# A streaming encoder layer: a third pair of score banks, one bank for turned weights, one for outputs, and sums made before the matmul

## The chip, the cores and the metric

The kernel runs on one core of a Trainium2 chip. The metric is the device time of one execution in microseconds, lower is better; 593.93 us is the median of three runs before the change. Of a core's engines, PE does matmuls (PEld are its weight loads), ACT activations and copies, DVE vector work, POOL further vector work and indirect transfers, SP issues most transfers. PE writes to PSUM, eight banks of 512 float32 columns in 128 partitions. Each engine runs its own program in order and waits on counts (semaphores) that the others raise.

## The reference, cut to what matters

```python
h = rmsnorm(x, g_mix); proj = h @ w_in            # GLU value and gate, q, k, v
a_out = silu(layernorm(causal_dwconv(u_hist, conv_w, conv_b), ln_g, ln_b))   # 512 channels, 31 taps
# stick-breaking attention, 8 heads of 64, blocks of 128 queries:
z = einsum(q, k) * scale
later = cumsum(log_keep, reverse=True) - log_keep   # log_keep = log sigmoid(-z) where visible
w = where(vis, exp(log_sigmoid(z) + later), 0);  o = w @ v
b_out = head_rmsnorm(o, g_sb)
x = x + concat(a_out, b_out) @ w_out
x = x + hier_moe(rmsnorm(x, g_ffn), ...)            # 32 experts
```

There are 528 prompt positions (16 learned ones and 512) and 32 new positions of a running stream with 1024 cached ones: with padding 576 columns. Keys and values of the prompt, of the new positions, and the last 30 convolution inputs are outputs too.

## The kernel before, in words

The input projection ends at about 143.7 us, the attention stage follows, and from about 248 us the output projection, the router and 32 experts.

**Attention steps.** `groups` (L415) lists 21 steps, s0 to s20; a step holds two heads. Group 0 is s0 to s3, 128 queries by 128 keys, two heads of the four blocks `i` each. Group 1 holds the few-query steps: s4 and s5 (the last 16 prompt queries: their own 32 keys, then 512), s6, s7 and s8 (the 32 new ones: their own, then twice 512 cached keys). Groups 2, 3 and 4 are s9 to s12 with 256 keys, s13 to s16 with 384, s17 to s20 with 512. `order` (L418) sets them in a row with three turns of keys for output (`ko`) and the three matmul parts of the LayerNorm (mean, variance, spread): 27 places, `q` = 0 to 26. All engines walk through these places.

**One step.** At its place PE makes scores (`scores`, L1013) into two banks; places use banks 0-1 and 2-3 in turn, so place q waits in `bank_free` for the weights of place q-2. ACT makes sigmoid(z) into SBUF and sigmoid(-z) in place (`shares`, L1558). DVE scans the second for the running products and multiplies (`weights`, L1886; the last product, L1908, frees the banks). Two places later (`TURN_LAG`) PE turns both heads' weights into banks 4 and 5 (`turn_weights`, L1042), ACT copies them to SBUF in one instruction (`copy_weights`, L1575), and three places later (`SUM_LAG`) PE multiplies them with the values into bank 6 or 7 (`weigh`, L1059). Four places after a group's last step ACT squares its outputs out of PSUM (`output_squares`, L1594) and DVE sums the squares by head (`head_means`, L1910); POOL makes the root (`head_root`, L741); six places after, DVE scales (`heads_normed`, L1916); seven after, PE turns the result (`turn_out`, L1088) and DVE takes it into the mixed input of the output projection (`outputs_in`, L1926), at the end of its place.

**Work beside it.** The convolution's taps are split: 98 by DVE (94 before the stage, one in each of the places 0 to 3), 26 by POOL (`tap`, L725). For POOL's, ACT makes the product (`product`, L1608), `PRODUCTS[q]` of them at place q, into four buffers: product n waits until POOL has used product n-4. `POOL_TAPS` says how many taps POOL makes before each of the first three head roots: 8, then 10, then 7, and one behind the third. The last four taps write the convolution's result `yc` (L738, L739). The mean (L1108) waits for all of them: eight matmul calls with a matrix of -1 sum four channel blocks in PSUM; DVE subtracts (L1871), ACT squares, 20 calls sum the squares by column (`variance`, L1118), POOL takes the root, PE spreads it, DVE scales (L1882), and at the place behind the last step ACT makes four Silus into the mixed input (L1634).

**The cached keys** are turned by PE at places 0 to 2 into banks 4 to 7 (`turn_ck`, L984) and copied by ACT and DVE, two blocks at a time.

**The way out.** At places 27 and 28 PE runs the first four blocks (attention's half, `LATE`) of the output projection of chunk 0, in two parts, between the last turns and weighings, then the other four, which need the Silus, then chunk by chunk. SP waits for the four Silus to load the first experts' weights, for the last weighing to load the router and more, and for w_out until s8 has been weighed.

## Time and profile before

| | |
|---|---|
| median of 3 runs | 593.93 us (593.9 to 594.14) |
| the profiled execution | 592.3 us, its span 590.6 us |
| mean granted clock of PE | 0.945 |
| PE, DVE, ACT, POOL busy | 527.3, 281.3, 155.7, 98.3 us |

In 40 slices of the span (14.77 us each; digits are tenths of busy time, 9 is 90% or more; PEclk the granted clock in tenths):

```profile
PE   6999999999767799899999799899999877988993
PEld 5779999999545568754555654344343322323330
DVE  2862999999687843714266851111112111001157
ACT  4513122223779832710211201111111111101112
POOL 2100000000657702011002111111112111011002
PEclk9999999999779885999999699999999999889997
DMA  8904745301504400069921789999999999999994
```

The tenth to the seventeenth slice hold the attention stage. A row of a timeline gives start, length, engine, line, operation, what it writes and reads, shape and count, and in brackets the idle time before it with what ended it. PE's matmuls of float32 appear as two passes each (eight calls, 16 passes); transposes as one.

### The profile page before, as it was taken

The numbers are of one execution on the slowest core, as the hardware profiler recorded it, in microseconds if no ns is written. First come the engines' busy times: TensorE is split into PE (matmuls) and PEld (weight loads), VectorE is DVE, ScalarE is ACT, GpSimd is POOL, SyncE is SP. The second block draws the span as 40 slices with busy tenths as digits, with TensorE's granted clock in tenths as the row PEclk, the third lists the DMA queues.
The fourth block names the chain that finished last, engine by engine and source line by source line (L and its number), as shares of the span: only waits on it lengthen the run. The fifth ranks groups of instructions, "written<-read, shape, count | busy, mean of one in ns | idle before, by whom it ended". The sixth has DMA issues, their size and how long they took to land.

```text
span 590.6 us, 7920 instructions
## 1 busy us (share of the span) xinstructions
PE 527.3 (89%) x3189; PEld 336.0 (57%) x3190; DVE 281.3 (48%) x481; ACT 155.7 (26%) x267; POOL 98.3 (17%) x120
## 2 busy tenths in 40 slices
PE   6999999999767799899999799899999877988993
PEld 5779999999545568754555654344343322323330
DVE  2862999999687843714266851111112111001157
ACT  4513122223779832710211201111111111101112
POOL 2100000000657702011002111111112111011002
PEclk9999999999779885999999699999999999889997
DMA  8904745301504400069921789999999999999994
GB/s 295 224 3 149 237 150 168 119 1 43 215 1 158 171 1 0 1 213 424 353 98 59 280 319 427 423 419 421 424 426 425 425 422 423 419 418 422 406 348 158
DMA packets 44764, 148.95 MB, mean 252 GB/s; under 512 B 7124, under 2 KB 23532, under 8 KB 36279
## 3 DMA queue, kind: packets, MB, share of 16 engines
q1 hardware_dynamic: 40263, 139.63, 61.2%
q0 software_dynamic: 4464, 8.80, 3.9%
q8 instruction: 26, 0.43, 0.3%
q14 instruction: 11, 0.09, 0.0%
HBM read 136.29 MB, written 19.59 MB: 264 GB/s over the span
## 4 chain that ended last, share of the span: by engine, by line
PE 60%; DMA 20%; DVE 8%; SPq 4%; issue 4%; ACT 3%; POOL 1%; DVEq 0%; POOLq 0%; ACTq 0%
PE ps L945 17%; DMA big<-in_w_expert_out 12%; PE ps L1170 9%; PE ps L1355 8%; PE ps L1380 5%; DMA cw<-h_dram,low 4%; PE ps L910 3%; PE ps L1071 2%; DVE ps L1895 2%; SPq L632 2%; DMA big<-y_dram 2%; PE ps L1336 2%; PE ps L1125 1%; DMA y_dram<-cw,low 1%; PE ps L898 1%
## 5 line engine op out<-in xcount | busy, mean ns | idle before, releaser
L2168 DVE TENSOR_TENSOR low<-low,ps 128x256 f32<-128x256 f32 x16 | 6.7, 421 | 172.0 <-ACT low L1688 172.0
L1355 PE MATMUL ps<-big,low 128*64 128x512 f32 x320 | 85.0, 593 | 3.3 <-issue 2.3
L945 PE MATMUL ps<-cw_r 128*128 128x280 f32 x256 | 72.3, 292 | 0.0
L1835 DVE SCALAR_TENSOR_TENSOR big<-low,cwt,big 128x590 f32<-128x590 f32 x94 | 72.1, 833 | 0.3
L945 PE MATMUL ps<-low_r,cw_r 128*128 128x280 f32 x256 | 72.2, 292 | 0.0
L945 PE MATMUL ps<-cw_r,big_r 128*128 128x280 f32 x256 | 72.1, 291 | 0.0
L1380 PE MATMUL ps<-big,low 128*64 128x512 f32 x160 | 47.0, 629 | 11.6 <-DMA big<-in_w_expert_out 4.8
L1170 PE MATMUL ps<-cw,low 128*128 128x512 f32 x128 | 56.7, 594 | 0.0
L1355 PEld LDWEIGHTS ps<-big,low 128*64 128x64 f32 x320 | 29.8, 137 | 45.6 <-issue 45.5
L736 POOL TENSOR_TENSOR big<-big 128x590 f32<-128x590 f32 x22 | 28.9, 1335 | 114.7 <-DVE big L1835 106.5
L945 PEld LDWEIGHTS ps<-cw_r 128*128 128x128 f32 x256 | 47.2, 188 | 0.4 <-issue 0.4
L945 PEld LDWEIGHTS ps<-cw_r,big_r 128*128 128x128 f32 x256 | 47.3, 188 | 0.0
L945 PEld LDWEIGHTS ps<-low_r,cw_r 128*128 128x128 f32 x256 | 47.2, 188 | 0.0
L1699 ACT ACTIVATE cw<-ps,low 128x1024 f32<-128x1024 f32 x16 | 17.8, 1115 | 98.2 <-PE ps L1380 98.2
L1355 PE MATMUL ps<-low 128*64 128x512 f32 x128 | 42.3, 593 | 0.2 <-issue 0.2
L1170 PEld LDWEIGHTS ps<-cw,low 128*128 128x128 f32 x128 | 23.6, 190 | 26.3 <-issue 26.3
L1688 ACT ACTIVATE low<-ps 128x256 f32<-128x256 f32 x16 | 6.2, 384 | 107.8 <-PE ps L1355 107.8
L716 POOL TENSOR_TENSOR stat<-stat,nhalf 128x1 f32<-128x1 f32 (+2 forms) x16 | 15.2, 953 | 114.4 <-DVE stat L2013 38.8
L1380 PEld LDWEIGHTS ps<-big,low 128*64 128x64 f32 x160 | 14.8, 144 | 31.6 <-issue 31.6
L798 POOL DMA_INDIRECT cw<-h_dram,low x16 | 16.5, 1034 | 94.7 <-PE ps L1336 83.1
L810 POOL DMA_INDIRECT y_dram<-cw,low x15 | 15.2, 1012 | 100.7 <-ACT cw L1699 87.3
L1895 DVE TENSOR_TENSOR_SCAN ps<-ps,negs 128x128 f32<-128x128 f32 (+4 forms) x36 | 25.4, 750 | 13.7 <-ACT ps L1573 8.9
(265 smaller groups left out, 829.3 us busy)
## 6 DMA issues: line engine op xcount, KB each, us to landing
big<-in_w_expert_in SPq DMA_DIRECT2D x16, 2048.0 KB, 18.1
big<-in_w_expert_out SPq DMA_DIRECT2D x20, 1024.0 KB, 25.3
big<-in_w_in SPq DMA_DIRECT2D x20, 512.0 KB, 5.1
low<-in_w_expert_out SPq DMA_DIRECT2D x8, 1024.0 KB, 29.8
low<-in_w_expert_in SPq DMA_DIRECT2D x4, 2048.0 KB, 22.3
cw<-in_w_expert_in SPq DMA_DIRECT2D x4, 2048.0 KB, 25.7
low<-in_w_expert_in SPq DMA_DIRECT2D x4, 1536.0 KB, 21.7
big<-in_w_expert_in SPq DMA_DIRECT2D x6, 1024.0 KB, 32.4
```

The lines of the kernel that those rows point to most:

```text
L716: pool.tensor_tensor(t, t, nhalf[0:t.shape[0], :].broadcast_to(list(t.shape)), ALU.pow).then_inc(rstd_ready, 1)
L736: pool.tensor_tensor(conv[:, i, :], t, conv[:, i, :], ALU.add).then_inc(pool_tap_done, 1)
L798: pool.indirect_dma_start(out=xg_of(g), out_offset=None, in_=h2_dram, in_offset=bass.IndirectOffsetOnAxis(ap=rows_of[:, g, 0:1].bitcast(U3 ...
L810: pool.indirect_dma_start(out=y_dram, out_offset=bass.IndirectOffsetOnAxis(ap=rows_of[:, g, 1:2].bitcast(U32), axis=0), in_=yg[b], in_offs ...
L910: mm = pe.matmul(ps[:, 4 + c % 2, :], h[:, k, cols], wts[:, k, :], start=m == 0 and k == 0, stop=m == 2 and k == KD - 1, skip_group_check= ...
L945: return pe.matmul(ps[:, proj_bank(j) + half, 0:PROJ], w[:, k, :], h[:, k, cols], start=first, stop=last, skip_group_check=True)
L1170: mm = pe.matmul(ps[0:w, OUT_BANK[c] + n, :], mixt[:, k, P * c:P * c + w], wout[:, k, 512 * n:512 * n + 512], start=k == LATE[0], stop=k = ...
L1355: mm = pe.matmul(ps[TILE * half:TILE * half + TILE, gu_bank(g), :], xt[:, k, TILE * half:TILE * half + TILE], wi_at(2 * g + half, k), star ...
L1380: mm = pe.matmul(ps[TILE * half:TILE * half + TILE, 4 + m, :], gact_t[:, k, TILE * half:TILE * half + TILE], wo[(2 * g + half) % WO_SLOTS] ...
L1699: act.activation((yg_end if g == PAIRS - 1 else yg[b]).rearrange("p (m n) -> p m n", m=2), ps[:, 4:6, :], ACT.Copy, scale=tab[:, g, 2:3]). ...
L1835: ins = dve.scalar_tensor_tensor(conv[:, i, :], u[:, i, j:j + CW], cwt[:, i, j:j + 1], conv[:, i, :], ALU.mult, ALU.add)
L1895: dve.tensor_tensor_scan(k, k, nones[:, 0:1].broadcast_to([P, n]), carry[:, a:a + 1] if cached else 1.0, ALU.mult, ALU.max).then_inc(left_ ...
```

## The change

What it does:

- A score place has three pairs of banks (0-1, 2-3, 4-5), `q % 3`: place q waits for place q-3. Bank 6 holds turned weights and turned outputs, bank 7 the outputs.
- The four turns of cached keys become places of their own, between s0 to s3: 31 places. New places: s0 to s3 at 0, 2, 4, 6, cached keys at 1, 3, 5, 7, `ko` at 8, 14, 19, s4 to s8 at 9 to 13, s9 to s12 at 15 to 18, s13 to s16 at 20 to 23, mean 24, s17 25, s18 26, variance 27, s19 28, spread 29, s20 30. In each such place ACT copies one block and DVE the other.
- Weights are turned three places behind, weighed four behind. With 384 or 512 keys a step's heads are turned one by one, each after the copy of the one before; ACT's copies come between its sigmoids, at the places behind the last step after the Silus.
- ACT copies a group's outputs from bank 7 to SBUF five places behind, and squares and scaling work there. Squares and their sums five behind, scaling seven, outputs eight, and `outputs_in` now comes ahead of the weights in DVE's place. The turn of outputs waits until all turned weights are copied; a turn of weights behind it waits until DVE has taken the outputs.
- DVE sums the four blocks of `yc`, and later of the squares, into one (`summed`); the mean is two matmul calls, the variance five.
- `POOL_TAPS` is (8, 9, 6), three taps stay behind the third root; `PRODUCTS` is one at places 0 to 13, then 2, 1, 1, 1, 1, 2, 1, 1, 1, 1.

```diff
 STEP_TAPS = 4
-POOL_TAPS = (8, 10, 7)
-PRODUCTS = (1, 1, 1, 1, 2, 1, 1, 2, 1, 1, 2, 2, 1, 2, 1, 2, 1, 1, 1, 1)
-TURN_LAG, SUM_LAG = 2, 3
-SQUARE_LAG, MEANS_LAG, NORM_LAG, OUT_LAG = 4, 4, 6, 7
+POOL_TAPS = (8, 9, 6)
+PRODUCTS = (1,) * 14 + (2, 1, 1, 1, 1, 2, 1, 1, 1, 1)
+TURN_LAG, SUM_LAG = 3, 4
+COPY_LAG, MEANS_LAG, NORM_LAG, OUT_LAG = 5, 5, 7, 8
+Z_SLOTS = 3
+TURN_BANK, O_BANK = 6, 7
...
         ln_mean, ln_var, ln_spread = dict(ln="mean"), dict(ln="variance"), dict(ln="spread")
-        order = groups[0] + [dict(ko=0)] + groups[1] + [dict(ko=1)] + groups[2] + [dict(ko=2)] + groups[3]
+        order = [entry for n, st in enumerate(groups[0]) for entry in (st, dict(ck=n))] + [dict(ko=0)] + groups[1] + [dict(ko=1)] + groups[2] + [dict(ko=2)] + groups[3]
         order += [ln_mean] + groups[4][0:2] + [ln_var, groups[4][2], ln_spread, groups[4][3]]
         NQ = len(order)
...
         for q, st in enumerate(order):
-            st["q"], st["bank"] = q, 2 * ((NQ - 1 - q) % 2)
+            st["q"], st["bank"] = q, 2 * (q % Z_SLOTS)
+        turned = 0
+        for st in steps:
+            st["turns"] = [(0, 1)] if st["n"] <= 256 else [(0,), (1,)]
+            st["turn"] = turned
+            turned += len(st["turns"])
+        NT = turned
         for g, sts in enumerate(groups):
             for n, st in enumerate(sts):
                 st.update(g=g, first=n == 0, last=n == len(sts) - 1)
         group_end = [sts[-1]["q"] for sts in groups]
-        O_BANK = (6, 7, 6, 7, 6)
...
-            def turn_weights(st):
-
-                s, n = st["s"], st["n"]
+            def turn_weights(st, part):
+
+                s, n, t = st["s"], st["n"], st["turn"] + part
                 pe.wait_ge(w_ready, s + 1)
-                if s:
-                    pe.wait_ge(wtt_ready, s)
+                if t:
+                    pe.wait_ge(wtt_ready, t)
                 else:
-                    pe.wait_ge(ckt_ready[0], 2)
+                    pe.wait_ge(qk_done, 8)
+                if part == 0 and st["turned_out"]:
+                    pe.wait_ge(mixb_ready, st["turned_out"])
                 w = wts[s % 4]
...
                 pe.wait_ge(onorm_ready, g + 1)
+                pe.wait_ge(wtt_ready, turned_before(g))
...
-                pe.wait_ge(yc_ready, NI)
-                pe.wait_ge(pool_tap_done, NI * TAPS - taps_by_dve)
-                for i in range(NI):
-                    for half in range(2):
-                        mm = pe.matmul(ps[:, st["bank"] + half, 0:HALF], nones[:, :], yc[:, i, HALF * half:HALF * half + HALF],
-                                       start=i == 0, stop=i == NI - 1, skip_group_check=True)
+                pe.wait_ge(sums_ready, 1)
+                for half in range(2):
+                    mm = pe.matmul(ps[:, st["bank"] + half, 0:HALF], nones[:, :], ysum[:, HALF * half:HALF * half + HALF],
+                                   start=True, stop=True)
                 mm.then_inc(mean_done, 1)
 
             def variance(st):
 
                 bank_free(st["q"])
-                for i in range(NI):
-                    pe.wait_ge(devsq_ready, i + 1)
-                    for c in range(NC):
-                        lo = min(P * c, COLS - P)
-                        mm = pe.matmul(ps[:, st["bank"], c:c + 1], lnsq[:, i, lo:lo + P], nones[:, 0:1],
-                                       start=i == 0 and c == 0, stop=i == NI - 1, skip_group_check=True)
+                pe.wait_ge(sums_ready, 2)
+                for c in range(NC):
+                    lo = min(P * c, COLS - P)
+                    mm = pe.matmul(ps[:, st["bank"], c:c + 1], sqsum[:, lo:lo + P], nones[:, 0:1],
+                                   start=c == 0, stop=True, skip_group_check=True)
...
+                early, late = step_at(q - TURN_LAG), step_at(q - SUM_LAG)
+                if early:
+                    turn_weights(early, 0)
+                if late:
+                    weigh(late)
+                if early and len(early["turns"]) == 2:
+                    turn_weights(early, 1)
...
-            def output_squares(g):
+            def copy_out(g):
 
                 act.wait_ge(av_done, groups[g][-1]["s"] + 1)
+                if g == 0:
+                    act.wait_ge(y_cleared, 16 * 9)
+                if g >= 2:
+                    act.wait_ge(o_turned, g - 1)
+                n = 256 if g == 1 else 512
+                o = ot if g == 1 else osb[g % 2]
+                act.copy(o, ps[:, O_BANK, 0:n]).then_inc(o_copied, 1)
+                act.wait_ge(o_copied, g + 1)
                 if g >= 1:
                     act.wait_ge(onorm_ready, g)
-                n = 256 if g == 1 else 512
-                act.activation(osq[:, 0:n], ps[:, O_BANK[g], 0:n], ACT.Square, scale=HD ** -0.5).then_inc(osq_ready, 1)
+                act.activation(osq[:, 0:n], o, ACT.Square, scale=HD ** -0.5).then_inc(osq_ready, 1)
...
-                if group_at(q - SQUARE_LAG) is not None:
-                    output_squares(group_at(q - SQUARE_LAG))
-                if step_at(q):
-                    shares(step_at(q))
-                    if q in (0, 1):
-                        copy_ck(2 * q)
+                if group_at(q - COPY_LAG) is not None:
+                    copy_out(group_at(q - COPY_LAG))
+                st, early = step_at(q), step_at(q - TURN_LAG)
+                if st and len(st["turns"]) == 1:
+                    shares(st, (0, 1))
+                elif st:
+                    shares(st, (0,))
                 elif q < NQ and "ko" in order[q]:
                     copy_ko(order[q])
+                elif q < NQ and "ck" in order[q]:
+                    copy_ck(order[q])
+                if early and q < NQ:
+                    copy_weights(early, 0)
+                if st and len(st["turns"]) == 2:
+                    shares(st, (1,))
...
-                if step_at(q - TURN_LAG):
-                    copy_weights(step_at(q - TURN_LAG))
+                if early and q >= NQ:
+                    copy_weights(early, 0)
+                if early and len(early["turns"]) == 2:
+                    copy_weights(early, 1)
...
+            def summed(total, t):
+
+                dve.tensor_reduce(total, t.rearrange("p i t -> p t i"), AX.X, ALU.add).then_inc(sums_ready, 1)
+
+            carried = [0]
             for q in range(NQ + OUT_LAG + 1):
                 if group_at(q - NORM_LAG) is not None:
                     heads_normed(group_at(q - NORM_LAG))
+                if group_at(q - OUT_LAG) is not None:
+                    outputs_in(group_at(q - OUT_LAG))
                 if step_at(q):
                     weights(step_at(q))
-                    if q in (0, 1):
-                        copy_ck(2 * q + 1)
+                elif q < NQ and "ck" in order[q]:
+                    copy_ck(order[q])
                 elif q < NQ and order[q] is ln_mean:
+                    dve.wait_ge(yc_ready, NI)
+                    dve.wait_ge(pool_tap_done, NI * TAPS - taps_by_dve)
+                    summed(ysum, yc)
                     deviations(order[q])
                 elif q < NQ and order[q] is ln_var:
+                    dve.wait_ge(devsq_ready, NI)
+                    summed(sqsum, lnsq)
                     variances(order[q])
                 elif q < NQ and order[q] is ln_spread:
                     normed(order[q])
```

## Rows read from the trace of the kernel before

**Rows 1.** Windows: us, engines' busy time (instructions), granted clock, DMA share, GB/s.

```profile
178.00:192.00 14.00, 10.30 (x193) 7.77 (x193) 9.99 (x16) 12.97 (x23) 10.52 (x10) 1.00 0.47 169
206.80:213.50 6.70, 6.70 (x18) 4.91 (x19) 0.00 (x0) 0.00 (x0) 0.00 (x0) 0.61 0.00 0
224.40:248.40 24.00, 22.20 (x139) 19.63 (x140) 13.32 (x14) 9.65 (x14) 3.08 (x3) 0.76 0.00 1
```

**Rows 2.** Waits, 143 to 250 us: us in total, times, longest.

```profile
DVE ps L1895 <- ACT ps L1573: 14.8, 6, 4.1
```

**Rows 3.** Timeline, from the scores of s20 into the first output projection.

```profile
241.97 1.13 PE L1019 MATMUL ps<-low 64*128 64x512 f32 x4
...
243.36 0.60 ACT L1572 ACTIVATE big<-ps 128x512 f32<-128x512 f32 x1 [3.77 <-PE ps L1022]
243.85 0.60 ACT L1573 ACTIVATE ps<-ps 128x512 f32<-128x512 f32 x1
...
246.41 1.28 ACT L1634 ACT_TABLE_LOAD   x1
...
246.44 2.00 PE L1071 MATMUL ps<-low,big 128*128 128x64 f32 x16 [1.80 <-ACT big L1582]
...
247.70 3.14 ACT L1634 ACTIVATE low<-big,vt 128x576 f32<-128x576 f32 x4
...
251.76 1.04 PE L1056 MATMUL ps<-ident,big 128*128 128x128 f32 x8
...
257.81 7.08 PE L1170 MATMUL ps<-cw,low 128*128 128x512 f32 x16
```

**Rows 4.** Timeline, from the last instruction of s16 to the deviations.

```profile
205.03 0.96 DVE L1908 TENSOR_TENSOR big<-ps,big 128x766 f32<-128x766 f32 x1
205.33 1.12 POOL L738 TENSOR_TENSOR big<-big 128x528 f32<-128x528 f32 x1
...
206.41 0.25 POOL L739 TENSOR_TENSOR big<-big 128x32 f32<-128x32 f32 x1
...
206.80 6.67 PE L1114 MATMUL ps<-big,negs 128*128 128x288 f32 x16 [1.01 <-POOL big L739]
...
213.50 2.75 DVE L1871 SCALAR_TENSOR_TENSOR big<-ps,big 128x576 f32<-128x576 f32 x4 [6.92 <-PE ps L1114]
```

**Rows 5.** Timeline of DVE: last instruction of s8, then of s12.

```profile
177.64 1.22 DVE L1908 TENSOR_TENSOR big<-ps,big 128x1022 f32<-128x1022 f32 x1
...
190.63 0.69 DVE L1908 TENSOR_TENSOR big<-ps,big 128x510 f32<-128x510 f32 x1
```

**Rows 6.** Lines of POOL: ns min/median/max, first and last start.

```profile
L736 POOL TENSOR_TENSOR big<-big x22: 1222/1334/1446, 148.9 to 194.2; 128x590 f32<-128x590 f32 x22
...
L746 POOL TENSOR_SCALAR stat_h<-stat_h x4: 240/241/245, 167.2 to 259.4; 128x8 f32<-128x8 f32 x4
...
L748 POOL TENSOR_TENSOR stat_h<-stat_h,nhalf x4: 1665/1666/1680, 167.5 to 259.7; 128x8 f32<-128x8 f32 x4
```

**Rows 7.** Groups of ACT by form in the attention stage.

```profile
L1613 ACT ACTIVATE big<-low,cwt 128x590 f32<-128x590 f32 x26 | 19.9, 789 | 0.0
...
L1582 ACT COPY big<-ps 128x512 f32<-128x512 f32 x4 | 2.3, 578 | 0.0
```

**Rows 8.** Lines of DVE: ns min/median/max, first and last start.

```profile
L1914 DVE TENSOR_REDUCE stat_h<-big x4: 675/676/687, 166.4 to 258.6; 128x8 f32<-128x512 f32 x4
L1914 DVE TENSOR_REDUCE stat_o<-big x1: 408/408/408, 188.4 to 188.4; 128x4 f32<-128x256 f32 x1
...
L2006 DVE TENSOR_TENSOR low<-x,low x10: 1068/1088/1100, 275.8 to 325.5; 128x512 f32<-128x512 f32 x8, 64x512 f32<-64x512 f32 x2
```

**Rows 9.** Timeline around the end of s18's weights.

```profile
218.73 2.39 ACT L1604 ACTIVATE big<-big 128x576 f32<-128x576 f32 x4
...
224.18 8.64 PE L1125 MATMUL ps<-negs,big 128*128 128x1 f32 x40
...
225.21 1.22 DVE L1908 TENSOR_TENSOR big<-ps,big 128x1022 f32<-128x1022 f32 x1
```

More of the change, by code:

```diff
@@ L437, in group_at, with turned_before @@
             return group_end.index(q) if q in group_end else None
+        def turned_before(g):
+            return sum(len(st["turns"]) for st in steps if st["q"] + TURN_LAG <= group_end[g] + OUT_LAG)
+        for st in steps:
+            st["turned_out"] = sum(end + OUT_LAG < st["q"] + TURN_LAG for end in group_end)
         def mixed(c):
@@ L1005, in bank_free @@
                     pe.wait_ge(ko_ready, gone["ko"] + 1)
+                elif "ck" in gone:
+                    for r in range(2):
+                        pe.wait_ge(ckt_ready[r], gone["ck"] + 1)
                 elif gone is ln_mean:
@@ L1060, in weigh @@
                 s, g, n, w = st["s"], st["g"], st["n"], wtt[st["s"] % 2]
-                pe.wait_ge(wtt_ready, s + 1)
-                if st["first"]:
-                    if g < 2:
-                        pe.wait_ge(ckt_ready[1], 2)
-                    else:
-                        pe.wait_ge(mixb_ready, g - 1)
+                pe.wait_ge(wtt_ready, st["turn"] + len(st["turns"]))
+                if st["first"] and g:
+                    pe.wait_ge(o_copied, g)
                 if "qb" in st:
@@ L1182, in _ @@
                         turn_ko(order[q])
+                    elif "ck" in order[q]:
+                        turn_ck(order[q])
                     elif order[q] is ln_mean:
@@ L1549, in _, with copy_ck, shares @@
                     upper(9 + 2 * i + HSLOTS)
-            def copy_ck(n):
-                b = 6 - 2 * n
+            def copy_ck(st):
+                n = st["ck"]
+                b = 7 - 2 * n
                 act.wait_ge(ck_turned, n + 1)
-                for a in range(2):
-                    ins = act.copy(ckt[:, :, P * b + P - P * a:P * b + 2 * P - P * a],
-                                   ps[:, 4 + a, :].rearrange("p (i t) -> p i t", i=NI))
-                ins.then_inc(ckt_ready[0], 1)
-            def shares(st):
+                act.copy(ckt[:, :, P * b:P * b + P],
+                         ps[:, st["bank"], :].rearrange("p (i t) -> p i t", i=NI)).then_inc(ckt_ready[0], 1)
+            def shares(st, heads):
                 s, n, bank = st["s"], st["n"], st["bank"]
-                act.wait_ge(z_ready, s + 1)
-                if s >= 4:
-                    act.wait_ge(w_turned, s - 3)
+                if 0 in heads:
+                    act.wait_ge(z_ready, s + 1)
+                    if s >= 4:
+                        act.wait_ge(w_turned, steps[s - 3]["turn"])
                 t = wts[s % 4][:, :, 0:n]
-                if n < 384:
+                if len(heads) == 2:
                     z = ps[:, bank:bank + 2, 0:n]
@@ L1569, in shares @@
                     return
-                for a in range(2):
+                for a in heads:
                     z = ps[:, bank + a, 0:n]
```

103 lines of the change are left out of this document (44 added, 59 removed).

## The prediction

> **What bounds the kernel now.** The page's forty slices show two parts: up to about 340 us PE works with little DMA, after that the experts' weights keep the DMA engines full. The change touches the attention stage between them, so I read three windows of it. From 178 to 192 us ACT is the full engine, 12.97 of 14.00 us; from 206.8 to 213.5 only PE works, 6.70 us; from 224.4 to 248.4 PE is busy 22.20 of 24.00 us, at a granted clock of 0.76 [rows 1]. So three limits follow one another, and each stretch is costed by its own. The waits show DVE standing 14.8 us in six waits for ACT's second sigmoid [rows 2]: the round trip through two pairs of banks, which the change goes for.
>
> What the end sees is when PE begins the second half of the first output projection, 257.81 us [rows 3]. From there PE runs projections, router and experts in a fixed order, and the weight loads wait for ACT's, PE's and DVE's counts of this stage. I take a shift of that point as a shift of the end, one to one. The sum is made against the profiled run, 592.3 us, 1.6 below the median of 593.93.
>
> **A, up to the weights of s16 (205.03 + 0.96 = 205.99 now) [rows 4].** I wrote the instructions of each engine one behind another in the new order, at their old durations, each no earlier than what it waits for. At first ACT loses: nine products of 0.7, not six, lie ahead of s4's sigmoids [rows 7], and the weights of s4 end some 1 us later. Then the third pair lets scores run ahead, so DVE no longer waits for a bank in the few-query steps. I place s8's weights at 175.4 us instead of 178.86, 3.4 earlier, and s12's at 188.8 instead of 191.32 [rows 5]; after that ACT, full already, sets the pace. This gain is eaten by POOL's root of the head norms. Product 12 (counting from 0) now stands at place 12 and needs a free buffer, so POOL's tap 8, which comes after the first root, which needs the sums of place 11. I place those at 165.75; root 0.4 + 1.67, tap 1.33 [rows 6]: 169.2. ACT arrives at 166.0 and stands 3.2 us, with s8's sigmoids behind it; that is in the 3.4. Product 21, at place 19, needs tap 17 behind the second root: sums 189.2, root some 1.5, tap 1.33 make 192.0; ACT arrives at 189.5 and stands 2.5, with s13's sigmoids behind it. What s12 had gained is gone; copies of outputs (five, 0.58 each at most [rows 7]) also go to ACT. Before, products 12 and 21 came later relative to the roots and hid behind them. A = 0, from -3 (no stands) to +2.
>
> **B, from there to the last deviation (213.50 + 2.75 = 216.25 now, 10.26 us) [rows 4].** Removed: the mean's eight matmul calls, 16 passes in the trace and 6.67 us, become two calls, four passes, 1.7 us at the same clock. Added: a DVE sum over 2304 elements ahead of it. And POOL has three taps left behind its third root, not one: its sums lie in s16's place, 0.68 us [rows 8]; root 0.4 + 1.67; three last taps 3 x (1.08 + 0.25), by their starts and ends [rows 4], 4.0. DVE stands there with everything behind it, PE stands at the mean.
> The sum's price: reductions of 512 and 256 elements took 0.676 and 0.408 us, 1.05 ns an element, which gives 0.14 + 2304 x 1.05 ns = 2.55 us. But the new one reads across the four blocks, each element 2304 bytes from the last. The one strided DVE row, 512 elements taken 32 bytes apart, took 1.09 us, 1.84 ns an element [rows 8]: 4.4 us. I take 4.4, since the stride is what it shares, and keep 2.55.
> The Trainium skill (SBUF — State Buffer, Door 1: The DMA port swizzle, its note on lines) says that an access which crosses into a new 16-byte line pays. By that rule the sum is the strided one, 4.4; without it the forecast would be 3.7 lower over both sums. The strided row agrees with it; no row shows a reduction at this stride.
> B = 0.68 + 2.07 + 4.0 + 4.4 + 1.7 + 2.75 + 0.4 of hand-overs = 16.0; change +5.8.
>
> **C, to the weights of s18 (225.21 + 1.22 = 226.43 now, 10.2 us) [rows 9].** After the mean PE turns half of s14, weighs s13, turns the other half and only then makes s17's scores: 12/16 of 2.00, two turns of 0.4 and 1.4 [rows 3], 3.7 at the full clock, up to 7.4 at half after PE's long stand; I take 4.6. Then ACT: two pairs of sigmoids (1.0 each by their starts [rows 3]), a copy of 0.5, the four squares of 2.39 [rows 9], another copy: 5.3, with the turn of s16 waiting for that last copy. At s18 the outputs of the third group are now taken in ahead of the weights on DVE. They need PE's turn, which needs the copy of s16's second head, last on ACT in that place: pairs and copies 2.9, turn 0.7, intake 0.8, then s18's own 3.6. After the mean 4.6 + 5.3 + 2.9 + 0.7 + 0.8 + 3.6 = 17.9; less the 2.85 of deviations, 15.05. Change +4.8. Of this about 3.7 is DVE standing with s18's sigmoids done.
>
> **D, to the end of s20's scores (243.36 now, 16.9 us) [rows 3].** Removed: 40 passes of the variance, 8.64 us, become 10, 2.2 us at the same clock [rows 9]. Added: the sum of 4.4 on DVE ahead of it. Then PE weighs s16 (1.5 at the full clock, 3.0 at half; 2.0) and makes s19's scores (1.4): 10.3 with hand-overs. To s20: two half turns, the spread, two half turns of s18, a weighing and scores, with waits for two copies: 7.5. D = 17.8; +0.9. So the variance's saving is spent.
>
> **E, to 257.81 (14.45 us now).** At the place behind the last step ACT makes the four Silus and only then copies s19's first half, now that turning is three places behind. PE can't turn the second half, nor begin the projection behind it, whose first four blocks need no Silu. So in a row: s20's sigmoids 2.1, table load 1.28, Silus 3.14, copy 0.58, half turn 0.5, copy 0.58, the turn of a group's outputs 0.6, projection 3.5, weigh s19 2.0, projection 3.5, then half turn 0.5, copy 0.7, half turn 0.5, copy 0.7, weigh s20 2.0 [rows 3, 7] = 22.2. Change +7.7. Before, the copies hid behind projection halves.
>
> **Free.** The stores and the w_out load on SP wait for the same counts and keep their order; w_out is asked for behind s8's weighing, long before its use. The wait for cleared rows moves from DVE to ACT, and those stores are long done. The cache blocks in the rotation are the same copies, one bank at a time. The last group's extra copy (0.58) lies beside a 7.08 us projection [rows 3].
>
> **Sum.** 0 + 5.8 + 4.8 + 0.9 + 7.7 = +19.2; 592.3 + 19.2 = 611.5, and 1.6 more for the median: **613 us**.
>
> **Rivals.**
> 1. *The POOL roots do not hold ACT or the sums back.* The place is products 12 and 21 and the last three taps; it decides if DVE runs as far ahead of ACT as ACT now runs ahead of DVE. Then A is -3 and up to 3 of B goes: 607. For it: which of ACT and DVE is ahead comes only from my placing. Against: each root needs DVE's sums of a place that ACT has just left.
> 2. *Contiguous price of both sums*: -3.7, 609. It can go with rival 1: 603.
> 3. *PE's clock in the tail.* PE stands some 5 us for the Silus. In 206.8 to 213.5, after a thin stretch, the granted clock was 0.61, partly its lower level [rows 1]. With the first projection half there at half clock, 3.5 more: 616; with C's at half too, 619. The Trainium skill (TensorE: Matmul & The Clock Gate, HAM oscillation) says that gaps in PE's work throw it back to 1.2 GHz; by it this is the likelier side, and the trace's low window agrees.
> 4. *Faster.* The place is the round trip of a score bank. If DVE's 14.8 us of waiting go [rows 2] and nothing takes their place, s16 ends as early as ACT's load allows, some 9 us; the mean comes at once behind it (B -1), DVE isn't held at s18 (C -4 of its +4.8), and the Silus' 5 us of E are hidden. -9 - 1 + 1 + 1 + 3 = -5: 589. It decides at product 12: if ACT does not stand there. The Trainium skill (Perfetto Trace Analysis, Matmuls) advises to rotate independent groups through banks, which speaks for it; here the third pair is paid for with a single bank for turned weights.
> 5. *The third pair is not used*, as PE comes to the next scores only behind a turn that waits for ACT, and the savings of mean and variance just pay for the rest: 594.
>
> **Chances.** Forecast 45%, rivals 1 and 2 together 25%, rival 3 20%, faster 7%, no change 3%. The range 602 to 620 leaves out the last two: low end both sums cheap and no stands (603, and 1 for rounding), high end the half clock in C and E (619) and 1. A measurement of this kernel can tell about 0.2%, 1.2 us. So faster 0.07, within 0.2% 0.02 (rival 5, a third of it falling to slower), slower 0.91.
>
> **What would show it.** Right: ACT idle ahead of a product until a POOL tap, twice; DVE idle about 6 us ahead of a new reduction, released by POOL; the reductions at 4.4 or 2.55 us; DVE idle ahead of the third group's intake in s18's place; PE idle some 5 us until the copy behind the Silus. The mean's matmuls near 1.7 us, the variance's near 2.2. Wrong: the second half of the first projection beginning before 258 us, or s16's weights ending before 200.

## The result, and the profile after

The changed kernel took 622.02 us (median of four runs, 620.14 to 624.26), 1.050 times the time of before (95% interval 1.042 to 1.059). Timed again after the experiments it was 1.054 [1.051, 1.057] of before; their ratios below are to be held against this one, and each carries about as wide an interval (0.3 to 0.5% to either side). The direction was forecast, the size was not: 613 us, with 620 as the upper end. The profiled execution took 620.14 us, 27.8 more than the one before.

Forty slices of the changed kernel:

```profile
PE   6999999997587364789999979999999978888994
DVE  2854999999766565600425674111211111111147
ACT  4421212226787441612011210101010000000012
PEclk9999999999978576877999959999999998889998
```

The attention stage now lasts into the nineteenth slice, and PE's clock is low through much of it (slices 12 to 19: 7, 8, 5, 7, 6, 8, 7, 7). The timeline at the ends of the five parts (last weights of s8, s12, s16, the deviations, the weights of s18, the first sigmoid of s20, the second half of the first projection; the last from a listing of PE alone, in which that half is one row):

```profile
174.75 1.22 DVE L1941 TENSOR_TENSOR big<-ps,big 128x1022 f32<-128x1022 f32 x1
...
189.72 0.69 DVE L1941 TENSOR_TENSOR big<-ps,big 128x510 f32<-128x510 f32 x1
...
207.66 0.95 DVE L1941 TENSOR_TENSOR big<-ps,big 128x766 f32<-128x766 f32 x1
...
221.91 2.75 DVE L1903 SCALAR_TENSOR_TENSOR big<-ps,big 128x576 f32<-128x576 f32 x4 [2.44 <-PE ps L1133]
...
237.98 1.22 DVE L1941 TENSOR_TENSOR big<-ps,big 128x1022 f32<-128x1022 f32 x1
...
257.98 0.60 ACT L1587 ACTIVATE big<-ps 128x512 f32<-128x512 f32 x1 [0.69 <-PE ps L1042]
...
283.84 9.62 PE L1188 MATMUL ps<-cw,low 128*128 128x512 f32 x16
```

Set against the same instructions of before [rows 3 to 5, 9], the shift grows so:

| part, up to | before | after | shift grown by | forecast |
|---|---|---|---|---|
| A, weights of s16 | 205.99 | 208.61 | +2.6 | 0 |
| B, last deviation | 216.25 | 224.66 | +5.8 | +5.8 |
| C, weights of s18 | 226.43 | 239.20 | +4.4 | +4.8 |
| D, first sigmoid of s20 | 243.36 | 257.98 | +1.9 | +0.9 |
| E, second projection half | 257.81 | 283.84 | +11.4 | +7.7 |
| behind it | | | +1.8 | 0 |

The stage itself began 0.7 us earlier in the changed kernel's execution (DVE's first scan at 144.58, before at 145.25), so counted from its start A grew by 3.3.

The stands that the prediction named are in the timeline; the bracket is the idle time ahead of a row and what ended it (two products on ACT, the first sum and the third group's intake on DVE, then the tail on ACT and PE):

```profile
169.18 0.79 ACT L1636 ACTIVATE big<-low,cwt 128x590 f32<-128x590 f32 x1 [2.87 <-POOL big L753]
...
193.42 0.79 ACT L1636 ACTIVATE big<-low,cwt 128x590 f32<-128x590 f32 x1 [2.21 <-POOL big L753]
...
215.42 4.05 DVE L1983 TENSOR_REDUCE big<-big 128x576 f32<-128x2304 f32 x1 [6.21 <-POOL big L756]
...
235.00 0.69 DVE L1965 TENSOR_TENSOR low<-ps,vt 128x512 f32<-128x512 f32 x1 [3.75 <-PE ps L1117]
...
260.08 1.28 ACT L1664 ACT_TABLE_LOAD   x1
261.38 3.14 ACT L1664 ACTIVATE low<-big,vt 128x576 f32<-128x576 f32 x4
264.42 0.56 ACT L1597 COPY big<-ps 128x512 f32<-128x512 f32 x1
...
265.13 1.09 PE L1079 MATMUL ps<-ident,big 128*128 128x128 f32 x4 [4.96 <-ACT big L1597]
266.98 1.09 PE L1117 MATMUL ps<-ident,big 128*128 128x128 f32 x4 [0.77 <-ACT big L1597]
267.86 5.59 PE L1188 MATMUL ps<-cw,low 128*128 128x512 f32 x8
...
281.18 2.86 PE L1091 MATMUL ps<-low,big 128*128 128x64 f32 x16 [0.68 <-ACT big L1597]
```

PE stands 4.96 us for the copy behind the Silus, and what follows is slow: a first projection half of 5.59 us where the second takes 3.65. Windows of the changed kernel around that stand (the column before the DMA share is the granted clock):

```profile
255.00:260.00 5.00, 5.00 (x41) 4.00 (x40) 5.00 (x6) 2.72 (x6) 1.90 (x2) 1.00 0.00 0
260.00:265.10 5.10, 0.17 (x2) 0.00 (x1) 2.90 (x3) 4.95 (x7) 0.00 (x0) 0.66 0.00 0
265.10:270.00 4.90, 4.11 (x11) 2.64 (x12) 0.69 (x1) 0.58 (x1) 0.00 (x0) 0.50 0.94 318
```

Full clock before the stand, the lower of the two levels behind it.

### The profile page after: what moved, and what is told of

It reads as the page before. It is cut to its first block, busy times and chain, and to the rows that moved or that the text cites. A ratio compares the mean times of both kernels' runs of the same rounds, so it can differ in the third digit from the quotient of the medians.

```text
span 618.4 us, 7874 instructions
## 1 busy us (share of the span) xinstructions
PE 526.7 (85%) x3147; PEld 329.9 (53%) x3148; DVE 292.8 (47%) x483; ACT 159.9 (26%) x283; POOL 99.4 (16%) x120
## 4 chain that ended last, share of the span: by engine, by line
PE 47%; DVE 20%; DMA 16%; ACT 6%; issue 5%; SPq 3%; POOL 2%; DVEq 0%; POOLq 0%; ACTq 0%
DMA big<-in_w_expert_out 12%; DVE big L1867 10%; PE ps L1188 10%; PE ps L1370 9%; PE ps L1395 6%; PE ps L962 4%; PE ps L927 3%; SPq L649 2%; PE ps L1091 2%; DMA cw<-h_dram,low 2%; PE ps L1351 1%; DVE ps L1927 1%; PE ps L1039 1%; DMA y_dram<-cw,low 1%; DVE big_r L1855 1%
## 5 line engine op out<-in xcount | busy, mean ns | idle before, releaser
L1370 PE MATMUL ps<-big,low 128*64 128x512 f32 x320 | 85.0, 594 | 1.6 <-DMA big<-in_w_expert_in 1.1
L1867 DVE SCALAR_TENSOR_TENSOR big<-low,cwt,big 128x590 f32<-128x590 f32 x94 | 73.5, 858 | 0.3
L1188 PE MATMUL ps<-cw,low 128*128 128x512 f32 x128 | 61.2, 633 | 0.0
L1395 PE MATMUL ps<-big,low 128*64 128x512 f32 x160 | 48.7, 643 | 11.7 <-DMA big<-in_w_expert_out 4.8
L1188 PEld LDWEIGHTS ps<-cw,low 128*128 128x128 f32 x128 | 25.5, 205 | 29.2 <-issue 29.1
L1079 PE MATMUL ps<-ident,big 128*128 128x128 f32 x104 | 19.2, 308 | 18.6 <-ACT big L1597 13.6
## 6 DMA issues: line engine op xcount, KB each, us to landing
low<-in_w_expert_in SPq DMA_DIRECT2D x4, 1536.0 KB, 22.2
```

Of the source, the lines that this page charges most:

```text
L1079: mm = pe.transpose(ps[:, TURN_BANK, lo + P * b:lo + P * b + P], w[:, a, P * b:P * b + P], ident[:, :])
L1188: mm = pe.matmul(ps[0:w, OUT_BANK[c] + n, :], mixt[:, k, P * c:P * c + w], wout[:, k, 512 * n:512 * n + 512], start=k == LATE[0], stop=k = ...
L1370: mm = pe.matmul(ps[TILE * half:TILE * half + TILE, gu_bank(g), :], xt[:, k, TILE * half:TILE * half + TILE], wi_at(2 * g + half, k), star ...
L1395: mm = pe.matmul(ps[TILE * half:TILE * half + TILE, 4 + m, :], gact_t[:, k, TILE * half:TILE * half + TILE], wo[(2 * g + half) % WO_SLOTS] ...
L1867: ins = dve.scalar_tensor_tensor(conv[:, i, :], u[:, i, j:j + CW], cwt[:, i, j:j + 1], conv[:, i, :], ALU.mult, ALU.add)
```

## The experiments

Each is an edit of the changed kernel unless its expectation names another base, timed in five rounds. The granted clock of a stretch differs from execution to execution (the part D took 18.8 us in both profiles of the changed kernel and 21.0 in those of e1 and e2, whose edits don't touch it), so a stage is read from its own start to its own end.

**The base again (e16).** No edit.

> No edit: the changed kernel once more, in the rounds of the experiments, as their common base. Theory (the edits' gains were read against the right base): ratio to the kernel before 1.047 to 1.053, E again some 25 us between s20's first sigmoid and the second projection half, with half clock behind PE's stand of 4.96 us. Rival (the four runs of the first comparison lay high): ratio 1.040 to 1.046, and every gain quoted from the ratios is 3 us smaller.

Measured: 624.63 us, 1.054 [1.051, 1.057]. Its trace repeats the stand of 4.96 us and an E of 25.85 us (258.02 to 283.87).

**E: the Silus' place (e1).**

```diff
-                if early and q < NQ:
+                if early:
                     copy_weights(early, 0)
+                if early and q == NQ:
+                    copy_weights(early, 1)
...
-                if early and q >= NQ:
-                    copy_weights(early, 0)
-                if early and len(early["turns"]) == 2:
+                if early and q != NQ and len(early["turns"]) == 2:
                     copy_weights(early, 1)
```

> Edit: at the place behind the last step ACT copies both halves of s19 before the four Silus. Theory (E is the Silus standing ahead of the copy, and PE's clock falling in the stand of 4.96 us): table load and Silus, 1.28 + 3.14 = 4.4 us, no longer hold PE, and the two turns and the first projection half behind it run at the full clock (1.09, 1.09 and 5.59 us become about 0.6, 0.6 and 3.6): 4.4 + 3.0 = 7.4 us less, about 614.6 us, PE's idle time ahead of the second half turn under 1 us. Rival 1 (only the hold, the clock is low there for another reason): 4.4 less, 617.6. Rival 2 (the Silus are needed by then, so the wait moves to the second projection half): 0 to 1 less.

Measured: 614.34 us, ratio 1.037 [1.033, 1.041]. PE's rows in its timeline:

```profile
263.19 0.63 PE L1079 MATMUL ps<-ident,big 128*128 128x128 f32 x4 [0.77 <-ACT big L1597]
...
265.05 3.60 PE L1188 MATMUL ps<-cw,low 128*128 128x512 f32 x8
```

The stand of 4.96 us is 0.77, the half 3.60 us; E is 18.6 us (260.23 to 278.85) in place of 25.9, 7.2 less, against 7.4 expected. Both rivals of the expectation fall.

**E: the stand without the clock (e2).**

```diff
+                if q == NQ:
+                    for _ in range(DUMMIES):   # 22
+                        pe.matmul(ps[:, 3, 0:P], ident[:, :], ident[:, :], start=True, stop=True)
                 if early and len(early["turns"]) == 2:
                     turn_weights(early, 1)
```

> Edit: the order of the Silus stays, but PE makes 22 extra matmuls of 128 x 128 into a free bank between the two half turns of s19 (22 x 0.21 = 4.7 us at the full clock, inside its stand of 4.96 us). They add work and change no result. Theory (the clock fell because PE stood): the stand is filled, the granted clock after it is 1.0, the turn, the turn of outputs and the first projection half take 0.6, 0.6 and 3.6 us instead of 1.09, 1.09 and 5.59: 3.0 less, about 619. Rival (the low clock has another cause, or the extra work delays PE): no change or up to 1 us more, 622 to 623.

Measured: 616.4 us, 1.041 [1.037, 1.045]. PE's rows:

```profile
262.81 5.08 PE L1217 MATMUL ps<-ident 128*128 128x128 f32 x44
...
269.80 3.60 PE L1189 MATMUL ps<-cw,low 128*128 128x512 f32 x8
...
282.96 7.08 PE L1189 MATMUL ps<-cw,low 128*128 128x512 f32 x16
```

Its windows, through the stand and behind it:

```profile
262.80:267.90 5.10, 5.09 (x46) 4.90 (x44) 2.67 (x3) 4.97 (x7) 0.00 (x0) 1.00 0.01 3
267.90:273.00 5.10, 4.29 (x16) 2.44 (x17) 0.69 (x1) 0.59 (x1) 0.00 (x0) 1.00 0.90 328
```

The Silus hold PE as long as before, but with 22 idle matmuls (44 passes) in the stand the granted clock stays at 1.00. E is 22.2 us (260.79 to 282.96), the very sum of the prediction, and the projection half behind it takes 7.08 us, not 9.62: 3.7 us of E and 2.5 behind it were clock alone. The theory holds; its 3 us left out the second fall, behind 280 us.

**B: taps behind the third root (e3).** `POOL_TAPS` is (8, 10, 7).

> Edit: POOL_TAPS is (8, 10, 7) again, so one tap, not three, lies behind the third root, and tap 17 lies ahead of the second root. Theory: the sum ahead of the mean comes two taps earlier (2 x 1.33 us, from the idle 6.21 us of DVE ahead of it), and ACT does not stand 2.21 us for product 21: 2.7 + 1 to 2.2 less, about 617 to 618. Rival 1: only the two taps show, 2.7 less, as PE and DVE set the pace between s12 and s16 whatever ACT does: 619.3. Rival 2: the earlier sum is spent waiting for another thing in the stretch behind the mean: under 1 less, 621 to 622.

Measured: 616.06 us, 1.040 [1.036, 1.045]. DVE's idle ahead of the sum is 3.47 us in place of 6.21, and no product stands at place 19. From s16's weights to the last deviation it takes 13.3 us, not 16.05 (the 2.7 expected). From s12's to s16's it takes 15.7, not 18.2; but e1 and e2, which leave this stretch alone, took 17.0 there, so the second stand is worth 1.3 to 2.5 us, about the theory's 2.2.

**A and B: no tap behind a root (e9).** `POOL_TAPS` is (12, 7, 7).

> Edit: POOL_TAPS is (12, 7, 7): the products of those taps are made ahead of the places whose sums the roots need, so that no root is delayed, no product waits for a tap behind a root, and no tap is left behind the third root. Theory (A's stands and B's wait are POOL's roots): ACT's stands of 2.87 and 2.21 us ahead of products go, DVE's idle 6.21 us ahead of the first sum goes too: 2.9 + 2.2 + 6.2 = 11 less at most, 611; at least the 6.2 and the second stand, 613.5. Rival 1 (the stand of product 12 is made good before s12 by a faster ACT anyway): 8.4 less, 613.6. Rival 2 (a root is now late, as it stands behind more taps): the turns of outputs and with them PE's next turns come late, 3 less or none, 619 to 622.

Measured: 610.25 us, 1.030 [1.026, 1.034]. In its timeline DVE's sum of s16's place follows at once:

```profile
205.30 4.04 DVE L1983 TENSOR_REDUCE big<-big 128x576 f32<-128x2304 f32 x1
...
211.78 2.75 DVE L1903 SCALAR_TENSOR_TENSOR big<-ps,big 128x576 f32<-128x576 f32 x4 [2.44 <-PE ps L1133]
```

The last deviation ends at 214.5, 10.1 us earlier: 3.8 in A, 6.3 in B. Yet s8's weights end no earlier (176.53, 175.97 with the stands): at s8 product 12's stand cost nothing, since DVE, not ACT, was behind. It held PE, though, which waits for ACT's copy of turned weights behind that product. PE and DVE in the changed kernel, from that wait to the scores, the intake and the scans of s9:

```profile
171.59 1.09 PE L1079 MATMUL ps<-ident,big 128*128 128x128 f32 x4 [5.03 <-ACT big L1597]
172.47 1.92 PE L1126 MATMUL ps<-ident,low 128*128 128x128 f32 x8
...
177.29 0.70 PE L1039 MATMUL ps<-low 64*128 64x256 f32 x4
177.40 0.69 DVE L1965 TENSOR_TENSOR low<-ps,vt 128x512 f32<-128x512 f32 x1 [1.43 <-PE ps L1117]
179.42 1.28 DVE L1927 TENSOR_TENSOR_SCAN ps<-ps,negs 128x256 f32<-128x256 f32 x2 [1.33 <-ACT ps L1583]
```

From 171.5 to 177 us the granted clock was 0.56: behind this stand too PE worked at its lower level (the turns of keys, L1126, took 1.09 us before). Without the stand s9's scores start at 174.19, though s12's weights end hardly earlier (190.13, 190.41). What slowed DVE is the next run.

**A: POOL's taps beside DVE (e13).**

```diff
-                    pool.tensor_tensor(conv[:, i, :], t, conv[:, i, :], ALU.add).then_inc(pool_tap_done, 1)
+                    pool.tensor_tensor(conv[:, i, 0:32], t[:, 0:32], conv[:, i, 0:32], ALU.add).then_inc(pool_tap_done, 1)
```

> Edit, on the changed kernel: POOL's taps but the last four add only 32 of 590 columns, so most of the convolution's POOL part is left out; ACT's products and every wait stay. Theory (A's miss is that DVE, full from 162 to 176 us, runs slower beside POOL's taps: 1.10 us for two columns at 168.06, 1.86 us for the scaling of heads at 170.40, where the same took 0.16 and 0.68 away from taps): these fall to 0.16 and 0.68, the two taps of 1.63 and 1.62 us at 147 and 151 to about 0.9, s8's weights end 2.5 to 3.5 us earlier, near 173; ACT's stands shrink by a tap each, 1.3 us; 616 to 619. Rival (the durations stay: it is the in-place operand, not POOL): s8's weights within 1 us of 176, 620 to 622.

Measured: 619.43 us, 1.046 [1.042, 1.050]; this kernel leaves out most of POOL's part of the convolution. DVE in the changed kernel, then with short taps:

```profile
151.14 1.62 DVE L1867 SCALAR_TENSOR_TENSOR big<-low,cwt,big 128x590 f32<-128x590 f32 x1
...
168.06 1.10 DVE L1933 TENSOR_TENSOR big<-big,stat 128x2 f32<-128x2 f32 x1
...
170.40 1.86 DVE L1953 TENSOR_TENSOR big<-big,stat_h 128x512 f32<-128x512 f32 x1
```

```profile
151.50 0.82 DVE L1867 SCALAR_TENSOR_TENSOR big<-low,cwt,big 128x590 f32<-128x590 f32 x1
...
167.62 0.16 DVE L1933 TENSOR_TENSOR big<-big,stat 128x2 f32<-128x2 f32 x1
...
169.02 0.68 DVE L1953 TENSOR_TENSOR big<-big,stat_h 128x512 f32<-128x512 f32 x1
172.26 1.22 DVE L1941 TENSOR_TENSOR big<-ps,big 128x1022 f32<-128x1022 f32 x1
```

The three durations fall to what they are away from taps. The Trainium skill (SBUF — State Buffer, Who interferes with whom) says that a DVE instruction with two SBUF inputs contends with a GpSimd instruction that reads SBUF; the three slowed instructions have two such inputs each, and the run agrees. The scans, whose long operand is in PSUM, kept theirs (2.46 us for two).

s8's weights end at 173.48, s16's at 206.35, where A = 0 had put them (206). But short taps do two things: DVE has its durations back, and the taps that ACT's two stands wait for are some 1.1 us shorter. Counted from DVE's first scan (144.58 in the changed kernel, 145.84 here), ACT's product 12 starts 2.9 us sooner: 1.7 are DVE's earlier sums ahead of POOL's first root, 1.1 the tap. s12's weights end 2.5 us sooner and s16's 3.5, the last 1.0 by the shorter stand for product 21 (1.23 us). What DVE gains at s8, 3.8 us, is not passed on: it then stands 2.65 us for PE ahead of the intake. So DVE's rate is about half of what this edit gives at s16; and e9, where the second and third of these rows still take 1.12 and 1.16 us and s8's weights end no earlier, takes 3.8 us out of A. That A's 2.6 us are DVE slowed beside POOL is not shown.

**C: the intake of outputs, last in its place again (e4).** The two lines of `outputs_in` move from ahead of `weights` to behind `head_means`.

> Edit: DVE takes a group's turned outputs at the end of its place again, behind the weights, not ahead of them. Theory: DVE's idle 3.75 us ahead of the third group's intake in s18's place goes, s18's weights end 3.7 to 4.5 us earlier: 3.7 less, about 618.3, idle ahead of the intake about 0. Rival: the turn of outputs holds PE's next turn of weights until the intake, which now comes later, so the stand moves from DVE to PE: 0 to 1 less, 621 to 622.

Measured: 620.78 us, 1.049 [1.045, 1.053], 0.5% under the base, with intervals that touch. The idle ahead of the intake is gone, and from s17's weights to s18's it takes 5.05 us, not 7.95: 2.9 of the 3.7. The end saw little of it in the profiled execution, since PE ran the stretch from the mean to s17's scores at its lower level:

```profile
229.96 1.23 DVE L1927 TENSOR_TENSOR_SCAN ps<-ps,negs 128x512 f32<-128x512 f32 x1 [3.84 <-ACT ps L1588]
```

That idle was 2.12 us in the changed kernel, where the clock rose earlier. It is not the edit's doing: from the last deviation to s17's weights took 8.3 us here and in e13, which leaves the intake alone, 6.6 in the changed kernel.

**The sums along the rows (e5).**

```diff
-                dve.tensor_reduce(total, t.rearrange("p i t -> p t i"), AX.X, ALU.add).then_inc(sums_ready, 1)
+                dve.tensor_tensor(pair, t[:, 0:2, :], t[:, 2:4, :], ALU.add).then_inc(dve_chain, 1)
...
+                dve.tensor_tensor(pair[:, 0, :], pair[:, 0, :], pair[:, 1, :], ALU.add).then_inc(sums_ready, 1)
```

> Edit: each of DVE's two sums is made by two adds along the rows (1152 elements, then 576) in place of one reduction across four blocks. Theory (the stride is what the 4.05 us pay for): at 1.05 ns an element, 1.3 + 0.75 us, 2.1 in place of 4.05, twice: 3.9 less, about 618. Rival 1 (a sum of 2304 elements of this kind has its price whatever the stride): two adds of two SBUF inputs take 3.5 us or more together, under 1 less, 621 to 622. Rival 2: the sum is shorter but the stretch behind it waits for another engine: 0 to 1 less with the adds at 2.1 us.

Measured: 618.88 us, 1.044 [1.040, 1.047]: the two adds take 1.36 and 0.76 us in place of 4.05, and B is 14.1 us in place of 16.05. The strided reduction's price is gone. How much of it was the stride and how much the operation, now two adds in place of one reduction, is not shown: no run reduced 2304 elements along the rows, for which 1.05 ns an element would make 2.55 us.

**Two pairs of banks (e7).** `Z_SLOTS` is 2.

> Edit: Z_SLOTS is 2, so places use two pairs of banks in turn again; all else is as changed. Theory (the third pair is what lets scores run ahead and takes DVE's waits for ACT away in the few-query steps): s8's weights end 3 to 6 us later than 176, s12's 1 to 4 later than 190.4; of that 2 to 5 us reach the end, 624 to 627. Rival (the third pair is not used, the order of PE's turns sets the pace): s8's weights within 0.7 us of 176, 621 to 623.

Measured: 627.45 us, 1.055 [1.050, 1.061], which the times alone do not tell from the base. The trace does: new waits of DVE for ACT stand in s3 (0.95 us) and s7 (2.14), and s8's weights end at 181.35. In this execution the stage began 1.5 us later (first scan at 146.07), ahead of what the edit touches; counted from there s8's weights end 3.9 us later than with three pairs, s12's and s16's 2.6, and the second projection half begins 2.1 later. The waits in s4 and s5 (2.54 and 1.37) were there with three pairs too (2.27 and 1.36). In the changed kernel the third pair is used, and rival 5 falls.

**Four edits together (e8).** e1, e9, e4 and e5.

> Edit: four edits at once: the copies ahead of the Silus, POOL_TAPS (12, 7, 7), the intake of outputs last in DVE's place, the sums as adds along the rows. Theory (each takes its own stand off one chain, so they add up): 8 + 11 + 3 + 4 = 26 less, about 596, near the kernel before. Rival 1 (they share stands: an earlier mean meets a PE at half clock all the same and the intake's stand is covered): 18 to 22 less, 600 to 604. Rival 2 (faster than before: the third pair's gain of 3 us in A shows now that nothing eats it): below 591.

Measured: 597.32 us, 1.007 [1.005, 1.010]. The theory's number is right to 1 us. By the ratios the four edits gave 1.7, 2.4, 0.5 and 1.0% one by one, 5.6% in all, and give 4.7% together; the difference is about what the intervals leave open, so four separate chains fit, and a small overlap is not ruled out.

**Sums on PE again, in the mended kernel (e12).** `mean` and `variance` as before, no `summed`.

> Edit, on top of three edits of e8_together (copies first, POOL_TAPS (12, 7, 7), intake last): DVE's two sums are left out and PE sums the four blocks again, eight calls for the mean, twenty for the variance. Theory (with adds along the rows DVE's sum is worth it): mean 16 passes at 0.41 to 0.565 us, 6.7 to 9.0 us, in place of 2.1 + 2.3; variance 8.6 in place of 2.1 + 2.3: 6.5 more than e8_together, 603 to 606. Rival (PE, kept busy by its own sums, stays at the full clock for what comes behind, which gives 3 to 4 us back): 599 to 601.

Measured: 600.03 us, 1.015 [1.011, 1.019], 0.8% more than with the adds, 2 to 7 us within the intervals: the rival's figure. Its mechanism is there too: behind its own mean PE is at full speed, and s17's weights end 5.5 us behind the last deviation, not 8.3 as in e8. In the profiles the second projection half begins 2.8 us later (265.95, 263.18).

**The mean behind the turns (e10).**

```diff
-                    elif order[q] is ln_mean:
-                        mean(order[q])
-                    elif order[q] is ln_var:
-                        variance(order[q])
...
+                if q < NQ and order[q] is ln_mean:
+                    mean(order[q])
+                elif q < NQ and order[q] is ln_var:
+                    variance(order[q])
                 if group_at(q - OUT_LAG) is not None:
                     turn_out(group_at(q - OUT_LAG))
```

> Edit, on top of the four edits of e8_together: in its two LayerNorm places PE makes the mean and the variance behind the turns and the weighing of the place, not ahead of them. Theory (behind the mean PE does at half clock what it could do while DVE still sums): turn, weighing and turn, 0.85 + 2.45 + 0.85 us, fall into PE's stand of 4.89 us ahead of the mean, and the weighing of 2.80 us into its 4.14 us ahead of the variance: 3.7 + 2.7 = 6.4 less, about 591. Rival (turn and weighing wait for ACT's copies there, or the mean comes later by as much): 0 to 2 less, 595 to 597.

Measured: 592.44 us, 1.001 [0.998, 1.004], by the ratios 3.5 us less, between the two: the mean follows the weighing without a stand, but the variance and s19's scores still take 2.27 and 2.08 us, half-clock prices.

**The tail (e11).** On top of it the calls of `project(0, ...)` move between the half turns, the last `turn_out` behind `project(1, LATE[0:4])`.

> Edit, on top of e10_mean_behind: the halves of chunk 0's projection stand between the two half turns of s19 and of s20, so that ACT's copies of turned weights hide behind them, and the last turn of outputs comes behind chunk 1's first part. Theory (in E four hand-overs of 0.77 us and the half turns lie bare): 2 to 4 less than e10_mean_behind, about 588, faster than the kernel before by 0.5 to 1%. Rival 1 (PE is in its stretch of a full row of matmuls behind it, and the later last turn of outputs holds DVE and so the router): equal or up to 3 more than e10_mean_behind. Rival 2 (the weight loads that wait for the last weighing come later and set the end): 1 to 3 more.

Measured: 589.92 us, 0.998 [0.996, 1.001]: 2 us, not told from the kernel before.

**Two pairs in the mended kernel (e14).** `Z_SLOTS` is 2 on top of that.

> Edit, on top of e11_tail_between: Z_SLOTS is 2, so that places use two pairs of banks in turn. Theory (the third pair is worth in the mended kernel what it was worth in the changed one, some 5 us, nearly all of it in the few-query steps): s8's weights end 4 to 6 us later than 177.2, the end 4 to 6 us later, 594 to 596. Rival (with no product standing, ACT sets the pace from s8 to s16 whatever DVE gained, as A said): s8 later, s16's weights within 1.5 us of 206.3, 590 to 591.

Measured: 591.46 us, 1.000 [0.997, 1.003]. s8's weights end 2.4 us later, s16's 1.1, s18's at the same time. The rival is right: here the third pair gives nothing that can be told.

**The squares one place later (e15).** In ACT's program `deviation_square` moves to the end of the place where `order[q - 2] is ln_mean`.

> Edit, on top of e11_tail_between: ACT makes the four squares of the deviations at the end of s18's place, not in s17's, so that the copy of s15's second head does not stand behind them. Theory (PE's stand of 1.81 us ahead of s16's turn is ACT's squares, and that stand is what puts PE at half clock from 218 to 231 us): the stand goes, s16's turn, weighings, variance and scores of s19 run at the full clock, s19's scores start 2 to 3 us earlier than 228.5: 586 to 588. Rival 1 (the clock is half there all the same): 0.5 to 1 less, 589. Rival 2 (DVE's second sum now waits for the squares): equal or 1 more, 590 to 591.

Measured: 588.16 us, 0.995 [0.992, 0.997], the one version faster than both kernels. PE's rows:

```profile
217.21 1.45 PE L1091 MATMUL ps<-low,big 128*128 128x64 f32 x12
222.15 2.26 PE L1143 MATMUL ps<-negs,big 128*128 128x1 f32 x10 [3.49 <-DVE big L1989]
224.34 2.08 PE L1039 MATMUL ps<-low 64*128 64x512 f32 x4
```

The stand of 1.81 us ahead of s16's turn is gone, and turn and weighing run at full speed (the weighing took 2.66). But PE, now early, stands 3.49 us for DVE's second sum, and behind that it is at half clock again. s19's scores start 4.2 us earlier than in the run before, e11 (224.34, 228.52), but 2.4 of that was there at the last deviation (211.72, 214.11), ahead of the edit. Its own part is 1.8 us, under the 2 to 3 expected; by the ratios the end comes 2 us earlier than in e11, with intervals that just touch.

## Why the prediction missed

The stands that it named were all there, and B and C had about their size. What it priced wrongly is the work behind a stand, in E above all, and in A.

- **B and C** came as worked out: 16.05 us against 16.0, 14.5 against 15.05. The strided reduction took 4.05 us (4.4 forecast, from the strided row), the stand for the intake 3.75 (3.7), that ahead of the first sum 6.21 (6). Rival 2 is out. Rival 1, that the roots do not hold, is out: product 21 stood 2.21 us, and product 12 stood 2.87, which s8 didn't feel, as DVE ended later than ACT there, but PE did.
- **E failed in one term**: the half turn, the turn of outputs, the first projection half and the last weighing behind PE's stand had the prices of the full clock. The stand itself came as forecast (4.96 us). At the lower level they made 25.9 us of 22.2, and the half behind it took 9.62 us, not 7.08, so that the shift did not reach the end one to one but grew by 1.8 more. That was rival 3, held at 20%, with its 3.5 us about right for E and nothing for what lies behind. The Trainium skill's rule (TensorE: Matmul & The Clock Gate, HAM oscillation), that gaps throw PE back to 1.2 GHz, spoke for it and was weighed too low; the trace agrees: 0.50 from 265.1 to 270.0 us, and 1.00 in e2, which fills the gap.
- **A failed in what a stand holds.** Product 12 started where it was placed (169.18; 169.2), yet s8's weights ended 0.6 us late (175.97; 175.4), s12's 1.6 (190.41; 188.8), s16's 2.6. At s8 it was DVE's "old durations": its rows beside POOL's taps took longer, and the scaling of heads, which read PSUM before, now has both inputs in SBUF. From there to s12 DVE was not what held: it stood 1.43 us for PE ahead of the intake. The prediction let product 12's stand hold only s8's sigmoids, but the copy behind it held PE 5.03 us, and PE's next work ran at 0.56. From 199 to 208 us it ran at 0.50 (0.65 before). That is E's term again, read from the rows and not tried: no run filled this stand alone, in e16 the level was low ahead of it already (0.50 from 166 us), and how the 2.6 us divide between PE's clock, DVE's rate and the length of the stands stays open.
- **Rival 4** had the third pair's gain too large. Counted from the stage's start, two pairs cost the changed kernel 3.9 us at s8 and 2.1 at the second projection half, and the mended one 2.2 at s8 and nothing that can be told at the end. Of DVE's 14.8 us of waiting [rows 2] only 5.95 lay in the few-query steps (3.81 and 2.14); 6.44 lay behind the mean.
- **D** was 1.0 off, with PE at 0.50 from 243.3 to 250 us; in e1 and e2, where the lower level lasted to some 257, D took 21.0 us, 2.2 more. In e15 the clock rose where a stand went and fell where one came; that D's 1.0 is just this was not tried by itself.

A, D, E and the projection behind it, 2.6 + 1.0 + 3.7 + 1.8, less 0.4 in C, are, to rounding, the 8.6 us by which the profiled execution stood above the sum.

## What to carry to other kernels

A stand is priced twice: its own length, and the lower clock of what PE does behind it, in E 4.96 us and then 3.7 + 2.5; so give PE work to do there, turns, weighings or half a projection, before its wait. Follow a stand to every engine that waits for it: the one that the prediction placed at product 12 held PE longer than it held the step it was priced for. When a change takes an engine's waits away, price its instructions anew at the rate they have beside the others, and then ask whether that engine is on the path. What a third buffer gives depends on what else sets the pace: here 3.9 us in the few-query steps of one version and 2.2 in another, and nothing that the time of either could tell.

## What the runs showed of the hardware

- A two-column DVE product took 0.16 us alone and 1.10 us beside a POOL tap (1.36 us on average): that looks like a wait for the tap's end rather than a slower rate, which was not tried apart.
- A reduction of 2304 float32 elements across blocks 2304 bytes apart took 4.05 us, 1.76 ns an element; two adds along the rows (1152 and 576 elements) did the same in 2.1.
- With the tail mended (e11) PE was at its lower level through 218 to 231 us, busy 11.86 of 13.00 us, behind a stand of only 1.81 us; in e15, without that stand, it was at full speed from 212 to 222 us. The window of e11 (granted clock 0.51):

```profile
218.00:231.00 13.00, 11.86 (x52) 9.81 (x53) 6.78 (x8) 4.00 (x9) 1.16 (x1) 0.51 0.00 1
```
